# The joins of a triangular block inverse cut down to their 32 and 64 wide blocks, and what moves around them

## The chip, the cores and the metric

One core of a Trainium2 chip runs the whole program. The metric is the time of one execution on the device in microseconds (us); the kernel before has a median of 1515.43 us in 3 runs (1513.37 to 1519.95).

## The reference, cut to what matters

One step of a diffusion backbone: width 1024, two layers, 512 latent tokens and 128 context tokens ("prompt") with the same weights. Layer 0 has a mixer: one input projection, a bidirectional gated DeltaNet with 4 heads of 128 beside a gated short convolution, one output projection. Layer 1 has a pooling mixer. Each layer ends in a gated ConvFFN. The adaLN vectors that modulate everything are `silu(cond) @ w_ada + b_ada`, for two conditions.

The part that the change touches is the triangular solve of the DeltaNet:

```
m = where(strict, einsum("bhncd,bhnsd->bhncs", kb, k) * decay, 0.0)
a = m + eye(CHUNK)
u = triangular_solve(a, vb);  w = triangular_solve(a, kb * exp(gc))
step: v_new = u - w @ s;  o = qg @ s + attn @ v_new;  s = s * gl + kg^T @ v_new
```

The kernel works in chunks of 128 tokens: 5 tiles (4 latent, 1 prompt), 2 directions, 4 heads, so it needs 40 inverses of unit triangular 128x128 matrices before its scan can start.

## The kernel before, in words

Everything is kept with channels on the partitions, tokens along the free axis. Large products are split in high and low parts: a **unit** is one 128 wide block of output channels, 48 matmuls of 128x320 (L686), and needs its weight tile loaded (SP queue, slots `raw`), rounded (`weight_hi` on ACT, L1114, or POOL) and its remainder (`weight_lo` on DVE, L1579, or POOL). The order of all work is written out by hand, one instruction stream for each engine, with semaphores between them.

The input projection is units 0 to 27: 8 of queries and keys, 12 of the short convolution, 4 of values (`U_V`), 4 of the gate (`U_G`, units 24 to 27). Between them DVE does the convolutions, the row sums (below), the products that fill `rinv` with the negated, masked gram matrices (`prepare`), and the inverses of all 32x32 diagonal blocks (`substitute`, L1695 and L1698: the two triangular factors of 4 blocks, 4 heads and all tiles side by side, 30 steps). This runs twice: the prompt's tile first (`lanes_out` at about 271 us), the four latent tiles after it (`lanes_out` at 309 to 313 us).

**The joins.** From the inverses of the diagonal blocks, the full 128x128 inverse comes in two steps, first 32 to 64 and then 64 to 128, as -D C D for each off-diagonal corner C. The kernel before does each with full 128x128 matrices, most of them zeros. ACT spreads the diagonal blocks into cleared buffers (`expand_pair`, 8 small copies per direction and tile, L1186). Then in each of 5 rounds (one tile or pair of tile and direction, both directions): `y5` (L835, 4 matmuls per direction), ACT copies the corners that count (`y5_copy`), `z5` (L845, L847, 8 matmuls), DVE adds (`update_t`, `update_r5`), `y6` (L854), `y6_copy`, `z6` (L862), DVE adds into `rinv` (`update_r6`). An fp32 matmul is two pairs of weight load and matmul instruction in the trace, so each round has 80 such pairs. Transposes of keys and values (`tokens`, L826, copied by ACT L1204) lie between them. The buffers are cleared by DMAs from a tensor of zeros, one of 2 MB.

**Row sums.** `row_sums(n)` (L1498) is the adaLN product for one row tile of 128 outputs: DVE multiplies a loaded 128x1024 tile by the two condition rows, two instructions with accumulation. `ROWS_IN`, `ROWS_B`, `ROWS_JOIN`, `ROWS_OUT` say how many stand where on DVE and `ROWS_LOAD` where their loads stand on the SP queue; a load waits until the sums two tiles earlier are done. Of the first 24, 10 stand in the input projection, 10 in the joins, 4 in the output projection.

**The scan** has 5 steps of both directions: products with the state (L903, L906), DVE (L1820), the product with `rinv` (L913), products with `kg` and the attention (L923, L925), and the state update. POOL scales the keys (`kg`, L646).

Of the kernel before, what the change touches and what calls it, by code (L numbers as in the profile page):

```python
# [26 lines left out]
P = 128  # L27
D = 1024
# [15 lines left out]
ADA_IN = 24  # L44
# [64 lines left out]
ROWS_LATE = ROWS_EARLY + ROWS_JOIN  # L109
assert ROWS_EARLY == 2 + sum(ROWS_LOAD.values()) and ROWS_LATE + sum(ROWS_OUT) == ADA_IN  # L110
# [3 lines left out]
PAIRS = [(NT - 1, 0), (NT - 1, 1)] + [(s if c == 0 else NT - 2 - s, c) for s in range(NT - 1) for c in range(2)]  # L114
# [31 lines left out]
def build(nc, t):  # L146
    ctx = ExitStack()
    with ctx:
# [46 lines left out]
        def heads(ap, n):  # L195
            return [ap[:, 512 * j:512 * (j + 1)].rearrange("p (h e) -> p h e", h=NH) for j in range(n)]
        rdx, ttx = heads(flat[:, 0:2048], 4), heads(flat[:, 2048:4096], 4)
        r5, tt2 = heads(flat[:, 4096:5120], 2), heads(flat[:, 5120:6144], 2)
# [5 lines left out]
        ys6 = nc.alloc_sbuf_tensor_at("ys6", [P, 2, NH, P], F32, offset=x_at + 13 * SLOT)  # L204
        sp_ = nc.alloc_sbuf_tensor_at("sp_", [P, 2, NH, P], F32, offset=x_at + 8 * SLOT)
        row_late = [nc.alloc_sbuf_tensor_at(f"row_late{j}", [P, SLOT], F32, offset=w_at + (2 + j) * SLOT * 4) for j in range(2)]
        cond_late = nc.alloc_sbuf_tensor_at("cond_late", [P, 2, D], F32, offset=w_at)
# [24 lines left out]
        ys5 = nc.alloc_sbuf_tensor_at("ys5", [P, 2, NH, P], F32, offset=o4)  # L232
# [8 lines left out]
        attn_kept = [attn[:, j] for j in range(2 * NT - 4)] + attn_last  # L241
# [124 lines left out]
        s_clear_r = sem("expanded_blocks_cleared")  # L366
        s_clear_y5 = sem("y5_products_cleared")
        s_clear_y6 = sem("y6_products_cleared")
# [4 lines left out]
        s_attn_work = sem("attn_moved_from_work")  # L373
# [3 lines left out]
        s_ex = sem("blocks_expanded")  # L377
# [3 lines left out]
        s_tt2 = sem("tt2_ready")  # L381
        s_r5 = sem("r5_ready")
# [3 lines left out]
        s_rinv = sem("rinv_ready")  # L386
        s_kq = [sem(f"scan_kq{c}") for c in range(2)]
# [26 lines left out]
        def row_buf(n):  # L414

            return (row_late[n % 2] if ROWS_EARLY <= n < ROWS_LATE else ada_raw[n % 2])[:]
# [5 lines left out]
        def row_cond(n):  # L422

            return cond_late if ROWS_EARLY <= n < ROWS_LATE else cond_rows
# [23 lines left out]
        def _(sp):  # L448
# [25 lines left out]
            for u in range(2, 28):  # L474
# [4 lines left out]
                if u == 3:  # L479
                    sp.wait_ge(s_x0, 8)  # L480
                    sp.dma_start(t["x_save"], x[:]).then_inc(s_saved, 16)
                elif u == 4:
                    sp.wait_ge(s_silu_rows, 1)
                    sp.dma_start(t["cond_save"], cond_rows[:]).then_inc(s_cond_saved, 16)
                elif u == U_B + 2:
                    sp.wait_ge(s_saved, 16)
                    sp.wait_ge(s_a, 8)
                    sp.dma_start(d_blk, t["zeros"][:, 0:SLOT]).then_inc(s_clear_d, 16)
                elif u == U_V + 2:
                    sp.wait_ge(s_bc, 2 * NT)  # L490
                    sp.wait_ge(s_row_sums, ROWS_EARLY)
                    sp.wait_ge(s_cond_saved, 16)
                    sp.dma_start(ys5[:].rearrange("p a h e -> p (a h e)"), t["zeros"][:, 0:SLOT]).then_inc(s_clear_y5, 16)
            sp.wait_ge(s_silu, PRIMED + NQKV)
            sp.wait_ge(s_am, 2 * NT)
            sp.dma_start(flat[:, 0:4096], t["zeros"]).then_inc(s_clear_r, 16)
            sp.wait_ge(s_ex, 2)
            sp.dma_start(ys6[:].rearrange("p a h e -> p (a h e)"), t["zeros"][:, 0:SLOT]).then_inc(s_clear_y6, 16)
# [4 lines left out]
            for j in (2, 1, 0):  # L503
                sp.dma_start(attn_kept[j], attn_first[j]).then_inc(s_attn_work, 16)
            sp.dma_start(cond_late[:], t["cond_save"]).then_inc(s_cond_rows, 16)
            for _ in range(2):
                load_rows(rows)
                rows += 1
# [4 lines left out]
            while rows < ROWS_LATE:  # L513
                load_rows(rows)
                rows += 1
            sp.wait_ge(s_ex, 2 * NT)
            sp.dma_start(x[:, 0:3], t["x_save"][:, 0:3]).then_inc(s_back[0], 16)
            sp.wait_ge(s_rinv, 2 * NT)
# [75 lines left out]
        def _(pool):  # L594
# [41 lines left out]
            pool.wait_ge(s_tok, 2 * NT)  # L636
            for s in range(NT):
                for c in range(2):
                    if s == 0:
                        pool.wait_ge(s_rinv, 2 * NT)  # L640
                    else:
                        pool.wait_ge(s_ap[c], s)
# [6 lines left out]
                if s == 0:  # L649
                    u = SEG["out"]["u"]  # L650
                    pool.wait_ge(s_row_sums, ROWS_LATE)
                    pool.wait_ge(s_cond_rows, 32)
# [23 lines left out]
        def _(pe):  # L676
# [120 lines left out]

            for u in range(28):
# [7 lines left out]
                if u == GSUM_AFTER:  # L806
                    gate_sums()
                if u in GRAMS_AFTER:
# [11 lines left out]
            def tokens(i, j):  # L820

                if i:
                    pe.wait_ge(s_tok, 2 * i + j - 1)
                c0 = TILES[PREP[i]]
                for h in range(NH):
                    last = nc.tensor.transpose(bank[6 + j][:, h], qkv[:, 4 + 4 * j + h, c0:c0 + P], ident)  # L826
                last.then_inc(s_tr, 1)

            def y5(l):
                n, c = PAIRS[l]  # L830
                pe.wait_ge(s_ex, l + 1)
                if l >= 2:
                    pe.wait_ge(s_y6c, l - 1)
                for h in range(NH):
                    last = nc.tensor.matmul(bank[c][:, h], rinv[:, 2 * n + c, h], ttx[l % 4][:, h],  # L835
                                            start=True, stop=True)
                last.then_inc(s_y5, 1)

            def z5(l):
                n, c = PAIRS[l]  # L840
                pe.wait_ge(s_y5c, l + 1)
                if l >= 2:
                    pe.wait_ge(s_rinv, l - 1)
                for h in range(NH):
                    nc.tensor.matmul(bank[2 + c][:, h], rdx[l % 4][:, h], ys5[:, c, h], start=True, stop=True)  # L845
                for h in range(NH):
                    last = nc.tensor.matmul(bank[4 + c][:, h], ys5[:, c, h], rdx[l % 4][:, h], start=True, stop=True)  # L847
                last.then_inc(s_z5, 1)

            def y6(l):  # L850
                n, c = PAIRS[l]
                pe.wait_ge(s_tt2, l + 1)
                for h in range(NH):
                    last = nc.tensor.matmul(bank[c][:, h], rinv[:, 2 * n + c, h], tt2[c][:, h], start=True, stop=True)  # L854
                last.then_inc(s_y6, 1)

            def z6(l):
                n, c = PAIRS[l]
                pe.wait_ge(s_y6c, l + 1)
                pe.wait_ge(s_r5, l + 1)  # L860
                for h in range(NH):
# [1220 lines left out]
```

## Time and profile before

| | us |
|---|---|
| median of 3 runs | 1515.43 |
| the profiled execution, own time | 1512.7 |
| its span | 1510.9 |
| TensorE (PE) busy in the span | 1403.6 (93%) |
| VectorE (DVE) busy | 989.8 (66%) |
| units 0 to 27 and what lies between them | 72 to 304 |
| joins, to the first matmul of the scan | 304 to 363 |
| scan | 363 to 417 |

The page gives PE 82% of the chain that ended last. Times in rows are microseconds from the start of the span. In a row of a timeline the first number is the start, the second the time from there to the end of the last instruction that is merged in it, x the count, and the bracket the idle time of the engine before it and what ended it. PEld is the weight load of TensorE, which overlaps the matmuls.

### The profile page before, as it was taken

How to read it: one execution, taken by the hardware profiler on the slowest of the kernel's cores; microseconds unless marked ns; L12 is line 12 of the kernel's file. 1: busy time of each engine (PE TensorE's matmuls, PEld its weight loads, DVE VectorE, ACT ScalarE, POOL GpSimd, SP SyncE). 2: the span in 40 equal slices, each digit the busy share in tenths (PEclk: the TensorE clock that was granted, in tenths of full speed). 3: DMA queues.
4: the chain of work that ended last, by engine and by line, in shares of the span. 5: the costliest groups of instructions: out<-in, count | busy, mean ns of one | idle time of the engine just before them, and what ended most of it. 6: DMA issues, size and time to landing. Idle time of an engine off the chain costs nothing.

```text
span 1510.9 us, 24566 instructions
## 1 busy us (share of the span) xinstructions
PE 1403.6 (93%) x9517; PEld 1366.8 (90%) x9517; DVE 989.8 (66%) x1403; ACT 428.9 (28%) x746; POOL 506.0 (33%) x304
## 2 busy tenths in 40 slices
PE   2699999989879799999999999888999999999996
PEld 1599989988879799999999999778999999999995
DVE  5784688887575777778888886446774155325554
ACT  4734443464421533102210222344110011001122
POOL 0200010003225133453356334112544545455442
PEclk9899999999989999999999999999999999999998
DMA  9342212353032235343434442111332222222222
GB/s 368 126 154 84 98 56 70 122 186 137 9 134 72 85 137 186 126 154 124 150 117 164 139 137 73 54 42 56 111 102 79 70 80 71 73 82 69 69 72 82
DMA packets 44791, 163.24 MB, mean 108 GB/s; under 512 B 4800, under 2 KB 5952, under 8 KB 43584
## 3 DMA queue, kind: packets, MB, share of 16 engines
q1 hardware_dynamic: 44736, 162.52, 31.2%
q8 instruction: 32, 0.52, 0.1%
q14 instruction: 23, 0.19, 0.0%
HBM read 154.12 MB, written 6.82 MB: 107 GB/s over the span
## 4 chain that ended last, share of the span: by engine, by line
PE 82%; DVE 8%; ACT 4%; issue 3%; DMA 2%; ACTq 0%; POOL 0%; DVEq 0%; SPq 0%; POOLq 0%
PE ps L686 72%; PE ps L971 1%; ACT work L1040 1%; ACT work L1186 1%; DMA x<-in_x 1%; PE ps L718 1%; PE ps L794 1%; DMA work<-in_zeros 1%; PE ps L925 1%; PE ps L923 1%; PE ps L913 1%; PE ps L764 1%; PE ps L698 1%; DVE work L1418 1%; DVE work L1478 1%
## 5 line engine op out<-in xcount | busy, mean ns | idle before, releaser
L686 PE MATMUL ps<-hhi,whi 128*128 128x320 f32 x1984 | 458.8, 312 | 31.8 <-DVE hlo L1482 29.9
L686 PE MATMUL ps<-hlo,whi 128*128 128x320 f32 x1984 | 454.0, 310 | 0.0
L686 PE MATMUL ps<-hhi,wlo 128*128 128x320 f32 x1984 | 453.4, 310 | 0.0
L686 PEld LDWEIGHTS ps<-hhi,whi 128*128 128x128 f32 x1984 | 333.5, 189 | 39.8 <-issue 17.8
L686 PEld LDWEIGHTS ps<-hlo,whi 128*128 128x128 f32 x1984 | 334.2, 189 | 0.0
L686 PEld LDWEIGHTS ps<-hhi,wlo 128*128 128x128 f32 x1984 | 334.0, 189 | 0.0
L603 POOL TENSOR_TENSOR wlo<-raw,whi 128x1024 fp32r<-128x1024 f32 (+1 forms) x102 | 255.4, 2504 | 8.5
L600 POOL TENSOR_SCALAR whi<-raw 128x1024 fp32r<-128x1024 f32 (+1 forms) x102 | 105.9, 1039 | 453.3 <-PE ps L686 360.5
L608 POOL TENSOR_TENSOR wlo<-raw,whi 128x1024 fp32r<-128x1024 f32 x44 | 110.7, 2515 | 213.7 <-ACT whi L1389 213.7
L686 PE MATMUL ps<-hidlo,whi 128*128 128x320 f32 x704 | 160.3, 308 | 0.0
L686 PE MATMUL ps<-hidhi,wlo 128*128 128x320 f32 x704 | 160.2, 308 | 0.0
L686 PE MATMUL ps<-hidhi,whi 128*128 128x320 f32 x704 | 160.2, 308 | 0.0
L1396 ACT ACTIVATE work<-ps 128x640 f32<-128x640 f32 x44 | 31.1, 706 | 428.7 <-PE ps L686 428.7
L1923 DVE TENSOR_TENSOR hidlo<-work,hidhi 128x640 fp32r<-128x640 f32 (+1 forms) x44 | 106.7, 2426 | 41.3 <-ACT hidhi L1406 41.3
L1515 DVE SCALAR_TENSOR_TENSOR work<-work,cols 128x511 f32<-128x511 f32 x120 | 122.1, 1058 | 3.7 <-DVE work L1512 0.3
L1512 DVE TENSOR_SCALAR work<-work,cols 128x640 f32<-128x640 f32 x60 | 60.2, 1003 | 97.0 <-ACT work L1396 79.6
L1498 DVE SCALAR_TENSOR_TENSOR ada_raw<-ada_raw,cond_rows 128x1024 bf16<-128x1024 f32 x70 | 121.6, 1738 | 0.0
L686 PEld LDWEIGHTS ps<-hidhi,wlo 128*128 128x128 f32 x704 | 117.8, 188 | 0.0
L686 PEld LDWEIGHTS ps<-hidlo,whi 128*128 128x128 f32 x704 | 117.8, 188 | 0.0
L686 PEld LDWEIGHTS ps<-hidhi,whi 128*128 128x128 f32 x704 | 117.7, 188 | 0.0
L1401 ACT ACTIVATE work<-work 128x640 f32<-128x640 f32 x44 | 32.5, 739 | 217.4 <-DVE work L1521 217.4
L1453 DVE SCALAR_TENSOR_TENSOR x<-ps,mod,x 128x320 f32<-128x320 f32 (+2 forms) x120 | 45.4, 434 | 70.6 <-PE ps L686 70.6
(202 smaller groups left out, 1411.0 us busy)
## 6 DMA issues: line engine op xcount, KB each, us to landing
raw<-in_w_gu SPq DMA_DIRECT2D x88, 512.0 KB, 3.2
ada_raw<-in_w_rows SPq DMA_DIRECT2D x70, 512.0 KB, 3.4
raw<-in_w_in SPq DMA_DIRECT2D x28, 512.0 KB, 3.3
raw<-in_w_dn SPq DMA_DIRECT2D x32, 448.0 KB, 3.3
ada_first<-in_w_ada SPq DMA_DIRECT2D x4, 2048.0 KB, 22.5
raw<-in_w_dn SPq DMA_DIRECT2D x16, 512.0 KB, 3.3
row_late<-in_w_rows SPq DMA_DIRECT2D x10, 512.0 KB, 3.3
raw<-in_w_out SPq DMA_DIRECT2D x8, 512.0 KB, 4.1
```

What stands on the lines that cost most here:

```text
L600: nc.gpsimd.tensor_scalar(whi[s][:, 0:n], raw[s][:, 0:n], 1.0, 0.0, ALU.mult, ALU.add).then_inc(s_whi, 1)
L603: nc.gpsimd.tensor_tensor(wlo[s][:, 0:n], raw[s][:, 0:n], whi[s][:, 0:n].bitcast(F32), ALU.subtract).then_inc(s_split, 1)
L608: nc.gpsimd.tensor_tensor(wlo[s][:], raw[s][:], whi[s][:].bitcast(F32), ALU.subtract).then_inc(s_split, 1)
L686: last = nc.tensor.matmul(pair[pr][:, b], wt[s][:, cs], act[:, k, b * HALF:(b + 1) * HALF], start=(j == 0 and q == 0), stop=(j == len(tile ...
L698: last = nc.tensor.matmul(ada_row(n), c_parts[:, q, 4 * s + k, :], w[:, k * ADA_COLS:(k + 1) * ADA_COLS], start=(s == 0 and k == 0 and q = ...
L1396: nc.scalar.activation(halves(pad[0]), pair["A"], ACT.Copy).then_inc(s_ev["A"], 1)
L1401: nc.scalar.activation(cv[1], cv[0], ACT.Silu).then_inc(s_silu, 1)
L1453: last = nc.vector.scalar_tensor_tensor(out=x[:, k, xc:xc + ln], in0=pair[n][:, bk, pc:pc + ln], scalar=mod[:, layer, 3 * part + 2, k, cd: ...
L1498: last = nc.vector.scalar_tensor_tensor(out=(row_out(n), row_buf(n)[:, 0:SLOT // 2].bitcast(mybir.dt.bfloat16))[c], in0=row_buf(n), scalar ...
L1512: own.tick(nc.vector.tensor_scalar(dst[:, 0:W], src[:, 0:W], taps[1], None, ALU.mult))
L1515: last = nc.vector.scalar_tensor_tensor(out=dst[:, c0 + 1:c0 + n], in0=src[:, c0:c0 + n - 1], scalar=taps[0], in1=dst[:, c0 + 1:c0 + n], o ...
L1923: nc.vector.tensor_tensor(hidlo[:, i, :], h32[0], hidhi[:, i, :].bitcast(F32), ALU.subtract).then_inc(s_hid, 1)
```

## The change

1. **Joins.** The matmuls multiply only blocks: `y5` and `z5` have 32x32 weights and 32 moving columns, `y6` and `z6` have 64 wide weights and 32 moving columns, in turn over 64 rows (the part that was just joined) and over 32 rows (the part that is still a single block). Each tile has 16 + 32 + 16 + 16 = 80 such matmuls for its 4 heads and 2 directions, where it had 40 full ones. Results of both directions and of two tiles stand in one bank. The tiles go in three groups, `JOINS`: the prompt's alone, then (0, 3), then (1, 2).
2. **No expansion, no zeros.** `expand_pair`, its cleared buffers, three DMAs of zeros and the adds go. In their place ACT and DVE copy joined rows and diagonal blocks beside each other (`even_rows`, `odd_rows`, `odd_diagonals`, `even_diagonals`), DVE copies finished parts into `rinv` (`inner_columns`, `outer_corner`), and POOL copies the 32 wide diagonals into it (12 copies, `s_rd`).
3. **Order.** The prompt's group goes between the gate units: `y5(0)` behind unit 24, `z5(0)` behind 25, `y6(0)` behind 26, `z6(0)` behind 27. The other two groups are interleaved with each other, with token transposes between them and six transposes behind them, all of which the scan's first matmul waits for.
4. **Row sums.** None stands in the joins any more: 18 in the input projection, 6 in the output projection, with the SP loads moved alongside, and the 10 loads, their buffers and a copy of the conditions in the joins go. Three attention tiles that were moved out of the work buffer stay where they are.

```diff
-ROWS_IN, ROWS_B = [0, 1, 1, 1, 1, 0, 1, 0], [1, 2, 2]
-ROWS_LOAD = {5: 1, 6: 1, 7: 1, 8: 1, 10: 1, 13: 1, 14: 1, 15: 1}
-ROWS_JOIN, ROWS_OUT = 10, [1, 1, 1, 1, 0, 0, 0, 0]
+ROWS_IN, ROWS_B = [0, 1, 1, 1, 1, 1, 1, 1], [2, 2, 1, 3, 2, 1]
+ROWS_LOAD = {4: 1, 5: 1, 6: 1, 7: 1, 8: 1, 9: 1, 10: 1, 11: 2, 12: 2, 13: 1, 14: 2, 15: 2}
+ROWS_OUT = [1, 1, 1, 1, 1, 1, 0, 0]
+JOINS = [(NT - 1,), (0, 3), (1, 2)]
+TOKENS = [(0, 0), (3, 0), (0, 1), (3, 1), (1, 0), (2, 0), (1, 1), (2, 1), (4, 0), (4, 1)]
...
+            def z5(g):
+                up, low = blocks_of(g)
+                y = join[g][0]
+                out = corner_bank(g).rearrange("p s (t h k) -> p s t h k", h=NH, k=BLOCK)
+                pe.wait_ge(s_y5c, g + 1)
+                for i, n in enumerate(JOINS[g]):
+                    for h in range(NH):
+                        for b in range(0, Q, 2):
+                            for c in range(2):
+                                to_, of = corner(c, b)
+                                r = (up, low)[c][quarter(to_), c, i, h]
+                                nc.tensor.matmul(out[quarter(to_), 1, i, h], r, y[quarter(to_), i, h],
+                                                 start=True, stop=True)
+                                last = nc.tensor.matmul(out[quarter(of), 0, i, h], y[quarter(to_), i, h], r,
+                                                        start=True, stop=True)
+                last.then_inc(s_z5, 1)
...
+            def y6(g):
...
+                for i, n in enumerate(JOINS[g]):
+                    for h in range(NH):
+                        for c in range(2):
+                            f = half(1 - c)
+                            a = rinv[:, 2 * n + c, h]
+                            nc.tensor.matmul(out[f, i, h, BLOCK * c:BLOCK * (c + 1)], a[half(c), f],
+                                             (q, p)[c][half(c), i, 1, h], start=True, stop=True)
+                            one = quarter(1 + c)
+                            last = nc.tensor.matmul(out[f, i, h, BLOCK * (1 - c):BLOCK * (2 - c)], a[one, f],
+                                                    (low, up)[c][one, c, i, h], start=True, stop=True)
+                last.then_inc(s_y6, 1)
...
+                if u >= U_G:
+                    (y5, z5, y6, z6)[u - U_G](0)
...
+            y5(1)
+            y5(2)
+            z5(1)
+            z5(2)
+            tokens(0)
+            tokens(1)
+            y6(1)
+            y6(2)
+            tokens(2)
+            tokens(3)
+            z6(1)
+            z6(2)
+            for j in range(4, 2 * NT):
+                tokens(j)
```

`y5` and `z6` are built like `z5` and `y6`. On DVE the new order is: `some_rows(2)` ahead of `weight_lo(10)`, 2, 1, 3, 2 and 1 sums behind it, one of them between `weight_lo(14)` and the first `scale_qk`; `even_diagonals(0)` behind the first `lanes_out`; `odd_rows(0)` behind `weight_lo(27)` and ahead of the last 17 steps of `substitute`.

## Rows read from the trace of the kernel before

**Rows 1.** Windows by stage: window, its length, busy us (count) of each engine, PEclk, DMA share, GB/s
```profile
72.00:304.00 232.00, 229.00 (x1509) 217.29 (x1509) 173.31 (x322) 95.31 (x173) 12.68 (x10) 1.00 0.29 98
304.00:363.00 59.00, 51.45 (x442) 49.86 (x441) 48.01 (x87) 35.34 (x105) 0.00 (x0) 1.00 0.47 161
```

**Rows 2.** Timeline of PE in the joins: the first waits, one round, the scan
```profile
304.85 2.02 PE L835 MATMUL ps<-work,rinv 128*128 128x128 f32 x16 [0.84 <-issue]
...
314.04 2.05 PE L854 MATMUL ps<-work,rinv 128*128 128x128 f32 x16 [3.15 <-DVE work L1714]
...
319.92 1.16 PE L835 MATMUL ps<-work,rinv 128*128 128x128 f32 x8 [0.50 <-ACT work L1186]
320.91 0.60 PE L826 MATMUL ps<-const,qkv 128*128 128x128 f32 x4
321.35 1.06 PE L845 MATMUL ps<-ys,work 128*128 128x128 f32 x8
...
362.98 1.13 PE L903 MATMUL ps<-ss,qkv 128*128 128x128 f32 x8 [1.35 <-issue]
```

**Rows 3.** The chain that ended last, in order of time: start, us, what
```profile
131.19 7.24 PE ps L686 x48
...
140.59 7.04 PE ps L686 x48
...
325.09 1.94 PE ps L854 x16
```

**Rows 4.** Timeline of PE around the transposes of 16 rows (L752)
```profile
130.33 0.46 PE L686 MATMUL ps<-hhi,wlo 128*128 128x320 f32 x2
130.72 0.48 PE L752 MATMUL ps<-const,work 16*128 16x16 f32 x5
131.12 0.56 PE L686 MATMUL ps<-hhi,whi 128*128 128x320 f32 x2
```

**Rows 5.** Timeline of the weight loads at the same place, and of the loads of L709
```profile
130.71 0.38 PEld L752 LDWEIGHTS ps<-const,work 16*128 16x128 f32 x5 [0.19 <-issue]
131.12 0.30 PEld L686 LDWEIGHTS ps<-hhi,whi 128*128 128x128 f32 x2
...
34.49 0.52 PEld L709 LDWEIGHTS ps<-cols,ada_rows 4*128 4x128 f32 x4 [0.23 <-issue]
```

**Rows 6.** Groups of weight loads by shape: busy us, mean ns of one
```profile
L835 PEld LDWEIGHTS ps<-work,rinv 128*128 128x128 f32 x80 | 9.6, 191 | 4.0 <-ACT work L1186 3.0 <-issue 1.1
L698 PEld LDWEIGHTS ps<-more,c_parts 128*4 128x4 f32 x64 | 4.8, 84 | 5.3 <-DVE more L1568 3.8
L752 PEld LDWEIGHTS ps<-const,work 16*128 16x128 f32 x5 | 0.4, 136 | 0.2 <-issue 0.2
```

**Rows 7.** Timeline of DVE and PE where the first grams wait
```profile
175.32 0.82 DVE L1632 TENSOR_TENSOR work<-work,ps 128x640 f32<-128x640 f32 x1 [6.35 <-PE ps L686]
182.35 1.23 DVE L1498 SCALAR_TENSOR_TENSOR junk<-ada_raw,cond_rows 128x1024 bf16<-128x1024 f32 x1
194.66 2.05 PE L794 MATMUL ps<-qkv 128*128 128x128 f32 x16 [2.55 <-DVE qkv L1624]
```

**Rows 8.** Timeline of DVE from the gate units to the end of the block inverses
```profile
273.86 1.22 DVE L1579 TENSOR_TENSOR wlo<-raw,whi 128x1024 fp32r<-128x1024 f32 x1
295.42 1.23 DVE L1579 TENSOR_TENSOR wlo<-raw,whi 128x1024 fp32r<-128x1024 f32 x1 [3.29 <-ACT whi L1114]
311.55 1.89 DVE L1705 STREAM_TRANSPOSE blocks<-blocks 128x1024 f32<-128x1024 f32 x1
```

**Rows 9.** Timeline of ACT and DVE: one token copy, the memsets ahead of the scan
```profile
321.68 0.60 ACT L1204 ACTIVATE ktok<-ps 128x512 f32<-128x512 f32 x1
365.22 1.03 DVE L1812 MEMSET sp__55<- 128x512 f32 x2
```

**Rows 10.** Timeline of DVE in the output projection; DMA issues: KB, us to landing
```profile
465.19 1.14 DVE L1453 SCALAR_TENSOR_TENSOR x<-ps,mod,x 128x320 f32<-128x320 f32 x3 [0.35 <-PE ps L686]
472.30 1.13 DVE L1453 SCALAR_TENSOR_TENSOR x<-ps,mod,x 128x320 f32<-128x320 f32 x3 [2.42 <-PE ps L686]
raw<-in_w_out SPq DMA_DIRECT2D x8, 512.0 KB, 4.1
```

More of the change, by code:

```diff
@@ new lines, in y6 @@
+            def y6(g):
+                up, low = blocks_of(g)
+                p, q = join[g][1:3]
+                out = join_bank(g, 2, 256).rearrange("p (t h k) -> p t h k", h=NH, k=64)
+                pe.wait_ge(s_ep, g + 1)
+                pe.wait_ge(s_eq, g + 1)
+                pe.wait_ge(s_pd, g + 1)
+                for i, n in enumerate(JOINS[g]):
+                    for h in range(NH):
+                        for c in range(2):
+                            f = half(1 - c)
[6 more added lines that the diff above has]
+                last.then_inc(s_y6, 1)
@@ new lines, in z6 @@
+            def z6(g):
+                up, low = blocks_of(g)
+                p, q, y = join[g][1:4]
+                out = join_bank(g, 3, 256).rearrange("p (t h k) -> p t h k", h=NH, k=64)
+                pe.wait_ge(s_y6c, g + 1)
+                for i, n in enumerate(JOINS[g]):
+                    for h in range(NH):
+                        for c in range(2):
+                            f, to_ = half(1 - c), half(c)
+                            nc.tensor.matmul(out[to_, i, h, BLOCK * (1 - c):BLOCK * (2 - c)], y[f, i, h],
+                                             (p, q)[c][f, i, 0, h], start=True, stop=True)
+                            one = quarter(2 - c)
+                            last = nc.tensor.matmul(out[to_, i, h, BLOCK * c:BLOCK * (c + 1)], y[one, i, h],
+                                                    (up, low)[c][one, c, i, h], start=True, stop=True)
+                last.then_inc(s_z6, 1)
@@ L850, in y6 @@
[L850 to L861, printed above, removed]
-                    last = nc.tensor.matmul(bank[4 + c][:, h], ys6[:, c, h], r5[c][:, h], start=True, stop=True)
-                last.then_inc(s_z6, 1)
+            y5(1)
@@ new lines, in even_diagonals, with odd_rows @@
+            def even_diagonals(g):
+                _, low = blocks_of(g)
+                dve.wait_ge(s_blk, 1 if g == 0 else 2)
+                for q in (0, 2):
+                    for c in range(2):
+                        nc.vector.tensor_copy(join[g][2][quarter(q), :, 1 - c], low[quarter(q), c])
+            def odd_rows(g):
+                dve.wait_ge(s_z5, g + 1)
+                for q in (1, 3):
+                    last = nc.vector.tensor_copy(join[g][2][quarter(q)].rearrange("p t s h k -> p s t (h k)"),
+                                                 corner_bank(g, quarter(q)).rearrange("p s (t e) -> p s t e", e=P))
+                last.then_inc(s_eq, 1)
```

355 lines of the change are left out of this document (165 added, 190 removed).

## The prediction

> **What bounds the kernel now.** The windows by stage come first [rows 1]. From 72 to 304 us PE is busy 229 of 232 us: the input projection is bound by PE. In the joins, 304 to 363 us, PE is busy 51.5 of 59.0 us at full granted clock, DVE 48.0, ACT 35.3. So the joins are a PE stage too, with some holes. The timeline of PE shows which [rows 2]: 0.84 us before the first join (so the last unit ends at 304.01), 3.15 us in the first round, 0.5 to 0.57 us in each of the four later rounds (one stands in the rows), and 1.35 us before the scan, which starts at 362.98. The chain of waits runs over PE's own matmuls in a round [rows 3]; DVE with its ten row sums and ACT with its expansions lie beside them. A change of the joins is therefore worth what it takes from PE's instructions and these holes, and not what it takes from DVE, ACT and the DMAs.
>
> **What one round costs PE now.** y6 of both directions, 16 pairs of weight load and matmul, takes 1.79 to 1.94 us [rows 3], 0.112 us a pair. A round has 80 such pairs, 8.9 us, and two token transposes of 0.44 us; five rounds are 44.6 us.
>
> **The joins in blocks.** The change doubles the number of matmuls: 80 for a tile, 160 pairs. Everything turns on two prices, and the trace of before has no 32 wide matmul.
>
> First the pair. The smallest matmuls that it has are the five transposes of 16 rows with 16 moving columns: their weight loads start within 0.38 us, and one lasts 0.136 [rows 5, 6], so the step is (0.38 - 0.136)/4 = 0.061 us. That is about 0.0625 us for a pair in which the matmul itself is tiny. Bound above: the full pair, 0.112 us. Bound below: the weight loads go from 84 ns for 4 columns to 191 ns for 128 [rows 6], 0.86 ns a column, so 32 columns take 28 ns; moving 32 columns where 128 need at most 112 ns also gives 28 ns. A pair can't be under 0.03 us, or 0.055 with 64 weight columns. I take 0.0625: it is the nearest row in size and the loads there already fetch few bytes.
>
> The Trainium skill ("TensorEngine Tiling (Array Packing)", Instruction Overhead) says that each matmul has an overhead of some 60 cycles, below which fewer columns gain nothing. By it an estimate from that page is 25 ns for each instruction of a pair at 2.4 GHz, 0.05 us a pair, a tile of 8 us without changes and 1499 us for the kernel; the step of 0.061 us in this trace speaks for more.
>
> Second the change of shape. Before the first 16-row matmul PE goes 0.24 us from the last start (two merged units start 0.147 apart, so the last at 130.48, then 130.72) instead of 0.147 [rows 4], and the weight loads show 0.19 us of idle put down to issue [rows 5]. The unit behind them takes 7.24 us instead of 7.04 [rows 3]. The stretch of the five costs 0.40 + 0.20 = 0.60 us; five steps of 0.0625 are 0.31; 0.29 is left for two changes. L709, with 4 rows, has the same idle time before its loads, 0.23 us [rows 5]. So changing between a full and a 32-row matmul costs 0.1 to 0.15 us. In the new y6 and z6, matmuls of 64 and 32 rows alternate: 32 changes for a tile. No row shows a change between these two; bounds 0 and 0.2 us, and I take 0.11, the low side of the measured one.
>
> The same page of the Trainium skill (Key Properties) says that a change of the tiling mode drains TensorE, while a change of tile does not. The rows around L752 agree with it, with 0.1 to 0.15 us each, and by it the alternation in y6 and z6 is charged.
>
> A tile then costs 160 x 0.0625 + 32 x 0.11 = 10.0 + 3.5 = 13.5 us of PE, against 8.9 before.
>
> **The prompt's group between gate units.** PE is full there [rows 1], so its 13.5 us push the end of unit 27 back one for one, with 8 changes between full and block shapes, 0.9 us: 14.4. It is not hidden, it is paid earlier. Its partners are in time: the first block inverse is out at about 271 us, y5(0) runs after 282, and every copy on ACT and DVE has a unit of 7 us to finish in.
>
> **The second block inverse.** It ends on DVE at 311.55 + 1.89 = 313.4 us [rows 8]. The 3.29 us in which DVE waited for ACT (held by the DMA of zeros) go; odd_rows(0) puts DVE behind z5(0), 0.6 us and some waiting. I get about 312, against 317 for PE's end of z6(0): PE is last. Were pairs at 0.03 us, this inverse would be last.
>
> **The rest of the joins.** Four tiles, 54.0 us. Tokens: twice two transposes, 0.9 us each time; six at the end with two banks, where a bank's next transpose waits for ACT's copy of 0.60 us [rows 9]: 3.5 us to the last one and 0.8 to its copy, 4.3 in all. Sum 60.1 us. ACT's and DVE's new copies, about 30 of 0.3 to 0.6 us, and POOL's 12 small ones, lie beside PE: with two groups interleaved each has a partner's matmuls as cover. Without it each of four hand-overs would add about 0.8 us. The scan's first step loses a stall: rr no longer queues behind a row sum and the memsets (365.22 for 1.03 us [rows 9], while kq of the first direction is done at about 364.8): -0.9.
>
> **Row sums.** In the input projection eight more sums of 2.3 us go into DVE's idle time before 175.32, of which the last piece alone is 6.35 us [rows 7]; their loads, 3.3 to 4 us to land, hold the SP queue behind the sums, but I find each weight tile landed at least 3 us before it is rounded. One tile fewer stands between the last weight_lo and scale_qk (now two, the second at 182.35): -2.3 us on the path to the grams, where PE waits 2.55 [rows 7]. The sums in front of body_conv(1) make it late by about 0.8: net -1.5. The four copies behind the first lanes_out push weight_lo(24), which has 0.8 us to spare (273.86 + 1.2, unit 24 begins at 275.8) [rows 8]: +0.3. Together -1.2, between -2.5 and +1. In the output projection two more sums fall into k = 4 and 5, where DVE has 0.35 to 2.42 us idle before an update [rows 10] and one add of squares that is stretched; PE needs raw tile 5 some 2 us later than it would then be split (4.1 us to land): 0, at worst +2. The DMAs that go, the expansions and the attention moves: 0, as their only stall on the path was DVE's 3.29 us.
>
> **Sum.** From 304.01: -1.2 + 14.4 + 60.1 = 73.3 us to the scan, against 59.0: +14.3, less 0.9 gives +13.4 us. On the profiled execution's own time, 1512.7 (span 1510.9), that is 1526.1; I say 1526. The median of the runs shown is 2.7 above that execution, so part of what is measured may be that.
>
> **Rivals.**
> A. Pairs at 0.0625 us, but a change between 64 and 32 rows is free. A tile is 10.0 us: -1.2 + 10.0 + 0.9 + 40.0 + 6.1 = 55.8 against 59.0, less 0.9: -4.1, 1509. For it: only changes from and to the full height are seen. Against: the 0.19 us of idle looks like a wait for the array to be empty, which two heights would need too. Pairs of 0.04 us with the changes charged end at the same place (6.4 + 3.5 = 9.9).
> B. The other side: the array's own time sets the step, and blocks in different corners overlap. y5 and z5 96 x 0.03, y6 and z6 64 x 0.055: 6.4 us a tile. PE would be done with the prompt at 310, the block inverse ends last at 312; then 25.6 + 6.1: the scan starts at 343.7, -19.3, less 0.9: -20.2, 1492.5. For it: full pairs run at what 128 columns take, and not above. Against: the step of 0.061 us for nearly nothing to multiply. The sign turns at a tile of (59.0 + 1.2 + 0.9 - 0.9 - 6.1)/5 = 10.8 us: stage of before, row sums, scan, less changes around the prompt's group and tokens.
> C. A pair costs the full 0.112 us whatever its size, as fp32 loads of 128 columns do: 17.9 + 3.5 = 21.4 a tile, +53 us, 1566. Milder: PE's clock is granted low for part of the joins because the array is mostly empty, +5 to +15 on top of the forecast.
>
> **How the numbers follow.** Forecast 0.44, A 0.22, B 0.22, C 0.12. The forecast's own range, with a tile of 12 to 15 us, is 1518 to 1534; the range for 8 in 10 takes in A, B's figure and the milder C: 1492 to 1542. What a measurement tells from no change is 0.5%, 7.6 us. Slower: C and most of the forecast, 0.12 + 0.38 = 0.50. Faster: B and a part of A, 0.22 + 0.09 = 0.31. Same: 0.19.
>
> **What would show it.** Step between weight loads in y5 and z5: 0.06 us (0.03 is B, 0.11 is C). In y6 and z6, if matmuls go by twos with about 0.23 us a two-pair product, the changes are paid; with 0.125, it is A. Group 0: behind the gate units stand 2.2, 4.2, 4.0 and 4.0 us of joins. Scan's start at 376 us; PE's wait before the first grams 1 us or less; no PE wait in units 4 to 7 of the output projection; PEclk at full in the joins. I am wrong if the joins after unit 27 take under 50 us.

## The result, and the profile after

The changed kernel takes 1535.45 us (median of 4 runs, 1533.46 to 1538.95) against 1516.49 for the kernel before on the same chip: 19.0 us slower by the medians, and a ratio of 1.0134 with a 95% interval of 1.0119 to 1.0149, which is 20.3 us. The sign and the range of the prediction hold; the size does not: 0.9% over 1512.7 was forecast with +13.4 us, and 19.0 came. (The forecast of 1526 us itself stands only 9.5 us above 1516.49, half of what came, since it was added to one execution that lay 3.8 us under that median.) The profiled execution after took 1538.95 us, 3.5 above its median, while the one before lay 3.8 below its own. The two traces are therefore 26.2 us apart where the medians are 19.0, and a figure that stands on the two traces alone is to be read with that in mind.

The row of the granted clock on the page, by slices of 38 us, first:

```profile
PEclk9899999955989999999999999998999999999998
```

Two slices of the 40 stand at 5 (307 to 384 us), where the joins are. The windows of this stretch (window, its length, busy us of each engine with counts, granted clock, DMA share, GB/s) answer to [rows 1]:

```profile
305.00:310.00 5.00, 5.00 (x25) 5.00 (x25) 4.46 (x16) 0.39 (x1) 0.00 (x0) 0.66 0.00 0
310.00:320.00 10.00, 10.00 (x204) 9.02 (x207) 9.18 (x18) 1.09 (x2) 3.64 (x8) 0.80 0.39 134
320.00:330.00 10.00, 6.23 (x276) 5.36 (x270) 4.20 (x10) 6.43 (x11) 0.00 (x0) 0.50 0.02 5
330.00:340.00 10.00, 10.00 (x59) 8.14 (x60) 0.87 (x3) 0.00 (x0) 0.00 (x0) 0.50 0.00 0
...
360.00:370.00 10.00, 10.00 (x59) 8.14 (x60) 1.38 (x2) 0.00 (x0) 0.00 (x0) 0.50 0.01 2
```

PE is never idle from 330 to 370 us (two of the four windows are shown), VectorE and ScalarE have next to nothing to do, and PE starts only 59 matmuls in 10 us, at 1.2 GHz (0.50) where the kernel before had 2.4 GHz throughout [rows 1]. The clock is already low at 305 to 310, in the unit behind y6(0), without any idle time before it. It is back at 1.00 when z6(0) starts (313.75), falls again inside z6(0) at 316, and stays at 0.50 until the scan.

The timeline of PE in y5(0), y6(0), y6(1), and at the end of the joins shows what a product costs (start, duration, line, names, shapes, machine matmuls merged in a row):

```profile
285.79 0.21 PE L830 MATMUL ps<-blocks,rinv 32*32 32x32 f32 x1
285.80 0.21 PE L830 MATMUL ps<-r_blk,rinv 32*32 32x32 f32 x1
...
286.05 0.19 PE L830 MATMUL ps<-r_blk,rinv 32*32 32x32 f32 x1
286.17 0.41 PE L700 MATMUL ps<-hhi,whi 128*128 128x320 f32 x1
...
301.33 0.30 PE L866 MATMUL ps<-work,rinv 64*64 64x32 f32 x2
301.56 0.30 PE L869 MATMUL ps<-blocks,rinv 32*64 32x32 f32 x2
...
335.76 0.42 PE L866 MATMUL ps<-work,rinv 64*64 64x32 f32 x2
336.10 0.41 PE L869 MATMUL ps<-rt_late,rinv 32*64 32x32 f32 x2
...
381.45 0.79 PE L965 MATMUL ps<-ss,qkv 128*128 128x128 f32 x5 [0.78 <-ACT vtok L1260]
```

The 32 pairs of y5(0) start within 0.26 us, 8 ns from one to the next. A product of y6 (one matmul of the program, two pairs in the trace) comes every 0.23 us at full clock and every 0.345 us at half clock. The scan starts at 381.45 us, 18.5 later than before [rows 2].

PE's waits before the scan (L808 are the first grams, L847 stands in z5) and, in a second view, in the output projection (us in all, times, longest):

```profile
PE ps L808 <- DVE qkv L1671: 3.8, 1, 3.8
PE ps L847 <- issue: 3.8, 2, 1.9
...
PE ps L700 <- POOL wlo L609: 4.6, 3, 2.7
```

The wait at the first grams is 3.8 us against 2.55 [rows 7], and behind it the grams run at a low clock: 16 matmuls in 3.79 us against 2.05. Unit 15 starts 2.3 us later than before. The timeline of VectorE shows why, and what became of the sums in the output projection:

```profile
166.57 1.23 DVE L1545 SCALAR_TENSOR_TENSOR junk<-ada_raw,cond_rows 128x1024 bf16<-128x1024 f32 x1 [2.07 <-DMA ada_raw<-in_w_rows]
...
183.03 2.06 DVE L1545 SCALAR_TENSOR_TENSOR ada_raw<-ada_raw,cond_rows 128x1024 bf16<-128x1024 f32 x1
...
479.75 2.06 DVE L1545 SCALAR_TENSOR_TENSOR junk<-ada_raw,cond_rows 128x1024 bf16<-128x1024 f32 x1
481.74 3.41 DVE L1545 SCALAR_TENSOR_TENSOR ada_raw<-ada_raw,cond_rows 128x1024 bf16<-128x1024 f32 x1
485.08 1.12 DVE L1500 SCALAR_TENSOR_TENSOR x<-ps,mod,x 128x320 f32<-128x320 f32 x3
```

VectorE waits for the row tiles themselves (2.07 us here, 2.67 at 175.04), and a half of a sum that takes 1.22 us elsewhere takes 2.06 to 3.41 here. GpSimd's two steps of a split, on its own timeline, are longer at the same time too, 1.69 and 3.24 us against 1.05 and 2.35 where no sum runs beside them:

```profile
479.05 1.69 POOL L606 TENSOR_SCALAR whi<-raw 128x1024 fp32r<-128x1024 f32 x1 [2.81 <-DMA raw<-in_w_out]
480.82 3.24 POOL L609 TENSOR_TENSOR wlo<-raw,whi 128x1024 fp32r<-128x1024 f32 x1
490.45 1.05 POOL L606 TENSOR_SCALAR whi<-raw 128x1024 fp32r<-128x1024 f32 x1 [6.39 <-DMA raw<-in_w_out]
491.58 2.35 POOL L609 TENSOR_TENSOR wlo<-raw,whi 128x1024 fp32r<-128x1024 f32 x1
```

The chain of waits in the output projection says who pays (start, us, what):

```profile
479.75 2.07 DVE junk L1545 x2
481.82 2.13 DVE ada_raw L1545
...
485.56 4.63 DMA raw<-in_w_out
```

SyncE holds the load of the next weight tile behind that of a row tile, which waits for the sum; GpSimd splits the weight late, and PE waits for the split. From the start of the scan to the end of the span the changed kernel takes 1155.8 us in this trace, the kernel before 1147.9.

### The profile page after: what moved, and what is told of

It is laid out like the page before. It is cut to its first block, busy times and chain, and to the rows that moved or that the text cites. A ratio compares the mean times of both kernels' runs of the same rounds, so it can differ in the third digit from the quotient of the medians.

```text
span 1537.2 us, 25228 instructions
## 1 busy us (share of the span) xinstructions
PE 1430.5 (93%) x9917; PEld 1380.1 (90%) x9917; DVE 990.2 (64%) x1409; ACT 404.4 (26%) x654; POOL 513.5 (33%) x316
## 4 chain that ended last, share of the span: by engine, by line
PE 83%; DVE 8%; ACT 3%; issue 3%; DMA 2%; POOL 0%; ACTq 0%; DVEq 0%; SPq 0%; POOLq 0%
PE ps L700 71%; PE ps L1033 2%; ACT work L1102 1%; DVE ada_raw L1545 1%; DVE junk L1545 1%; PE ps L883 1%; PE ps L886 1%; PE ps L866 1%; PE ps L869 1%; PE ps L808 1%; PE ps L732 1%; PE ps L922 1%; DMA x<-in_x 1%; DMA ada_raw<-in_w_rows 1%; PE ps L987 1%
## 5 line engine op out<-in xcount | busy, mean ns | idle before, releaser
L1545 DVE SCALAR_TENSOR_TENSOR ada_raw<-ada_raw,cond_rows 128x1024 bf16<-128x1024 f32 x80 | 139.9, 1748 | 0.0
L1545 DVE SCALAR_TENSOR_TENSOR junk<-ada_raw,cond_rows 128x1024 bf16<-128x1024 f32 x80 | 99.7, 1246 | 6.4 <-DMA ada_raw<-in_w_rows 4.7
```

What stands on the lines that cost most here:

```text
L1545: last = nc.vector.scalar_tensor_tensor(out=(row_out(n), row_buf(n)[:, 0:SLOT // 2].bitcast(mybir.dt.bfloat16))[c], in0=row_buf(n), scalar ...
```

## Experiments

All numbers are against the kernel before, run on the same chip in between. Kernels of one group of four shared these runs. The medians: by_shape 1503.74, by_head 1511.14, same_corner 1545.05, rows_only 1520.79 (before 1516.32); fill_waits 1498.61, fill_all 1507.69, tokens_early 1501.63, rows_back 1495.18 (before 1516.29); after_fill 1538.9, after_rows 1530.04, best 1495.49, best_late 1491.45 (before 1514.93).

### The order of the two shapes: by_shape and by_head

```
y6 and z6, by_shape:
+ for part in range(2):                # 0: 64 rows, 1: 32 rows
      for i, n in enumerate(JOINS[g]):
          for h in range(NH):
              for c in range(2):
                  ... the product of this part alone
by_head: for i / for h / for part in range(2) / for c
```

> The changed kernel with the products of y6 and z6 in another order: first all those of 64 rows, then all those of 32 rows (two shapes, one change between them in each function, in place of one at every product). Nothing else moves. Theory, that the alternation of the two shapes is what the joins pay for, by itself (0.2275 us a product of two pairs at full clock) and by a granted clock of 0.50 that follows it: y6(0) falls from 3.65 us to about 1, y6 and z6 of the two groups from 22 us each to 4 to 8, the clock no longer falls at 305 to 310, and the kernel takes 25 to 45 us less than the changed one (1490 to 1510). Rival, that pairs of 64 and 32 rows cost this much by themselves and the clock falls because of the waits for VectorE in the joins: under 3 us less, still 0.23 us a product.

> The changed kernel with y6 and z6 taken per head: two products of 64 rows, then two of 32 rows, so half the changes of shape. Theory (each change of shape has a price): y6(0) about 2 us in place of 3.65, the two groups' y6 and z6 10 to 15 us each in place of 22, the kernel 10 to 22 us under the changed one. If the price were the pair's and not the change's: no change in time. If only the low clock mattered and it needs fewer changes to come: between the two, with the clock at 0.50 and a product that costs no less.

by_shape: 1503.74 us, ratio 0.9926 (0.9907 to 0.9944), 31.7 us under the changed kernel and faster than the kernel before. by_head: 1511.14, ratio 0.9973 (0.996 to 0.9985), 24.3 under the changed kernel, a little more than the upper end of 22 that was expected. PE's timeline of y6(0) in by_shape:

```profile
301.98 0.66 PE L869 MATMUL ps<-work,rinv 64*64 64x32 f32 x16
302.56 0.24 PE L872 MATMUL ps<-blocks,rinv 32*64 32x32 f32 x1
...
303.14 0.56 PE L700 MATMUL ps<-hhi,whi 128*128 128x320 f32 x2
```

The same 32 pairs take 1.16 us with one change of shape in place of 3.65 with 15, so 14 alternations cost 2.49 us, 0.18 us each, if what neighbours of one shape gain by overlapping (the 32-row pairs here lie in two corners and start by twos) is put down to them. by_head stands between: with 7 changes its y6(0) takes 1.87 us (301.83 to 303.70), so the first six more cost 0.12 us each and the last eight, which also part the pairs of neighbours, 0.22. The mean is therefore not the price of a change alone. The windows of by_shape:

```profile
305.00:310.00 5.00, 5.00 (x36) 5.00 (x35) 4.49 (x16) 0.00 (x0) 0.00 (x0) 1.00 0.00 0
310.00:320.00 10.00, 5.22 (x316) 4.74 (x315) 9.47 (x21) 3.98 (x7) 3.66 (x8) 0.65 0.40 134
320.00:330.00 10.00, 7.82 (x210) 7.16 (x194) 5.07 (x12) 4.14 (x7) 0.00 (x0) 0.50 0.02 4
330.00:340.00 10.00, 10.00 (x154) 9.41 (x154) 1.34 (x2) 1.79 (x3) 0.00 (x0) 0.50 0.01 3
```

The clock no longer falls behind y6(0). It still falls at 313, where PE waits 3.1 us for the second block inverse behind z6(0) (from 311.6 to 314.7), and stays low until 347. At half clock y6 of the two groups takes 7.4 us (325.55 to 332.94) and z6 7.4, against 22.2 each; in by_head they take 11.3 each. The rival, that pairs of these shapes are dear by themselves, falls.

### Neighbours in one corner: same_corner

```
y5 and z5:
- for i, n in enumerate(JOINS[g]): / for h / for b / for c
+ for b / for c / (z5: for part) / for i, n in enumerate(JOINS[g]): / for h
```

> The changed kernel with the 32-row products of y5 and z5 ordered so that all products of one 32x32 corner of the array stand in a row (in the changed kernel neighbours lie in different corners, 8 to 15 ns from start to start). Theory, that neighbours in different corners overlap: the step grows to 30 to 60 ns, 448 products more by 0.02 to 0.05 us each, together 9 to 20 us over the changed kernel. Rival, that a product of 32 rows and 32 columns is this short wherever it lies: the same time within 2 us. Since z5's two products of a pair stand apart here, the order inside z5 changes too.

1545.05 us, ratio 1.020 (1.018 to 1.022), 9.6 us over the changed kernel, at the low end of the theory. y5(0) begins and ends:

```profile
286.30 0.34 PE L830 MATMUL ps<-blocks,rinv 32*32 32x32 f32 x5
...
286.88 0.32 PE L830 MATMUL ps<-r_blk,rinv 32*32 32x32 f32 x5
287.12 0.56 PE L700 MATMUL ps<-hhi,whi 128*128 128x320 f32 x2
```

The unit behind it starts 0.82 us after y5(0) in place of 0.38: 32 pairs are 0.44 us, or 14 ns each, dearer, so some 22 ns from one to the next in place of 8. The 9.6 us hold more than is seen at once: the two holes of PE in z5 (3.8 us in the changed kernel) are gone, so the dearer pairs cost more than 9.6. Neighbours in different corners of the array do overlap; this is rival B's mechanism, at a price well under its 30 ns. The Trainium skill ("TensorEngine Tiling (Array Packing)", Instruction Overhead) has some 60 cycles for each matmul, 25 ns as an estimate from that page. Counted once for a pair it is near the step of 22 ns within one corner; counted for each instruction of a pair, as the prediction did (0.05 us), it is too much, and the 8 ns between corners lie under it either way.

### The row sums alone: rows_only and after_rows

```
rows_only, against the kernel before:
- ROWS_IN, ROWS_B = [0, 1, 1, 1, 1, 0, 1, 0], [1, 2, 2]
- ROWS_JOIN, ROWS_OUT = 10, [1, 1, 1, 1, 0, 0, 0, 0]
+ ROWS_IN, ROWS_B = [0, 1, 1, 1, 1, 1, 1, 1], [2, 2, 1, 3, 2, 1]
+ ROWS_JOIN, ROWS_OUT = 0, [1, 1, 1, 1, 1, 1, 0, 0]
after_rows, against the changed kernel (5 rows in two buffers of the weight parts, free then):
+ ROWS_IN, ROWS_B = [0, 1, 1, 1, 1, 1, 1, 1], [2, 2, 1, 2, 1, 0]
+ ROWS_JOIN, ROWS_OUT = 5, [1, 1, 1, 1, 0, 0, 0, 0]
  ...            # in both kernels the loads of the rows move alongside
  inner_columns(2)
+ some_rows(4)
  outer_corner(1)
+ some_rows(1)
```

> The kernel before with the row sums alone placed as in the changed kernel (none in the joins, more before the first grams and two more in the output projection, the shift added at the seventh row). Theory from the changed kernel's trace: slower than the kernel before by 6 to 10 us, of which 2 to 3 before unit 15 (sums that wait for their rows and then run at 2 us beside GpSimd) and 6 to 7 in the output projection (sums of up to 3.4 us in front of the weight splits). Rival, the forecast (row sums hidden in slack): 0 to 3 us faster.

rows_only: 1520.79 us, ratio 1.0028 (1.0016 to 1.0039), 4.5 us over the kernel before. PE's waits, for GpSimd in the output projection and for VectorE at the first grams:

```profile
PE ps L680 <- POOL wlo L599: 4.4, 2, 2.8
...
PE ps L788 <- DVE qkv L1618: 3.6, 1, 3.6
```

Before they were 1.6 and 2.55 us. By the traces unit 15 starts 2.2 us later than before (200.71 against 198.52), the joins 2.3 later (307.15 against 304.85), the scan 1.6 later (364.60), and from there to the end of the span it takes 3.6 us more. So the 2 to 3 us before unit 15 came as expected, and of the 6 to 7 in the output projection about half. The theory had 6 to 10 us, from the trace of one execution of the changed kernel; the cost is real, and smaller. The forecast of a gain falls.

> The changed kernel with the row sums placed as in rows_back and nothing else: the joins' y6 and z6 alternate as in the changed kernel. Theory (the placement of the row sums costs its own part, whatever the joins do): 6 to 10 us under the changed kernel, as rows_back lay 8.6 under by_shape. Rival, that the 4.5 us that rows_only showed are all there is: 4 to 5 under. If the sums' loads delay the joins, under 3.

after_rows: 1530.04 us, ratio 1.0105 (1.0079 to 1.0131), 5.4 us under the changed kernel by the medians, 4.4 by the ratios. That fits the rival, which took the 4.5 us of rows_only for all there is. The wait at the first grams is gone and the one for GpSimd is back at 1.6 us, but PE's holes in z5 grow from 3.8 to 6.5 us, and the unit behind y6(0) takes 9.8 us where it took 8.8, since the clock falls earlier; so what the two projections win is partly lost again in the joins.

### What brings the clock down: fill_waits, fill_all, after_fill

```
+ fill(12)     # matmuls 128 x 128 x 512 into a free bank, their result is not used
  y5(1)
  y5(2)
+ fill(4)
  z5(1)
+ fill(8)
  z5(2)
+ fill(8)
fill_all: also fill(2) before each block of 8 products of y6 and z6
after_fill: the fills of fill_waits in the changed kernel
```

> The kernel by_shape with matmuls that serve nothing (128 rows and columns, 512 elements, into a bank that is free then) in PE's waits of the joins after unit 27: 12 before y5(1), 4 before z5(1), 8 before z5(2), 8 behind it. In by_shape the granted clock falls to 0.50 at 312 us, in a wait of 3.1 us behind z6(0), and stays there to 347. Theory, that the clock falls because the array has too little full-size work in these microseconds: it stays at 1.00 until 325 at least, and the time falls by 3 to 12 us (if y6 and z6 too then run at full clock, by some 12; if the clock falls inside them, by 3). Rival, that the small shapes alone bring the clock down, whatever stands between them: 0.50 from 312 on all the same, and the time is the same or up to 6 us more.

fill_waits: 1498.61 us, ratio 0.9893 (0.9874 to 0.9911), 5.1 us under by_shape. Its windows:

```profile
310.00:320.00 10.00, 8.38 (x308) 6.63 (x307) 9.61 (x21) 4.14 (x8) 3.65 (x8) 1.00 0.39 134
320.00:330.00 10.00, 9.29 (x252) 7.87 (x252) 4.97 (x12) 3.89 (x7) 0.00 (x0) 1.00 0.02 6
330.00:340.00 10.00, 9.76 (x184) 8.75 (x183) 3.72 (x6) 3.50 (x7) 1.91 (x6) 0.83 0.11 19
```

The clock stays at 1.00 through y6 and most of z6, for work that is of no use: the theory holds. y6 takes 4.2 us and z6 4.5 in place of 7.4 each.

> The kernel fill_waits with two more such matmuls ahead of each block of 8 products of y6 and z6 of the two groups (16 blocks, 32 matmuls of some 0.22 us at full clock, 7 us in all). Theory (full-size work holds the clock): 1.00 through the joins, so that their 7.1 us each for y6 and z6 come down to 3.5 and the ten token groups to half, 12 us gained against 7 paid: 2 to 6 us under fill_waits if the clock falls there in y6, 5 to 8 over it if it held there already. Rival (small shapes bring it down anyway): 0.50 all the same, 12 to 15 us over by_shape.

fill_all: 1507.69 us, ratio 0.9946 (0.9926 to 0.9966), 9.1 us over fill_waits by the medians and 8.0 by the ratios, at the upper end of the 5 to 8 expected for a clock that was held already. The additional matmuls cost their time and more changes of shape: a block of 8 products comes every 1.25 us, 0.59 of it its own.

> The changed kernel, its y6 and z6 still alternating between 64 and 32 rows, with the 32 matmuls that serve nothing of fill_waits in PE's waits of the joins. It parts the two costs of the alternation. Theory (each change of shape costs its price, and the low clock comes from too little full-size work): the clock is at 1.00 where the joins begin; if it stays there, the 64 products each of y6 and z6 take 0.2275 us in place of 0.345, 15 us less than the changed kernel's, about 1520. If the alternation itself brings the clock down again inside y6 (as at 305 in the changed kernel, behind y6(0)), only 2 to 6 us less, 1530 to 1534. If the fillers did nothing: 0 to 6 more.

after_fill: 1538.9 us, ratio 1.0164 (1.0137 to 1.019): 3.5 us over the changed kernel by the medians, 4.5 by the ratios. None of the gains came; the time is that of fillers that do nothing, though the trace shows that they did something. Its windows, and two products at full clock:

```profile
320.00:330.00 10.00, 9.19 (x406) 7.14 (x405) 2.50 (x4) 5.58 (x10) 0.00 (x0) 1.00 0.02 6
330.00:340.00 10.00, 10.00 (x75) 8.16 (x74) 2.56 (x9) 1.14 (x3) 0.00 (x0) 0.82 0.01 2
340.00:350.00 10.00, 10.00 (x59) 8.13 (x59) 0.00 (x0) 0.60 (x1) 0.00 (x0) 0.50 0.00 0
```
```profile
334.15 0.30 PE L869 MATMUL ps<-blocks,rinv 32*64 32x32 f32 x2
334.38 0.30 PE L866 MATMUL ps<-work,rinv 64*64 64x32 f32 x2
```

The same fillers that hold the clock in front of products in order bring it to 1.00 here too, up to 336 us; then it falls to 0.50 inside the alternating products of y6, with PE busy all the time and no wait before it. So the alternation costs twice: 0.23 us a product, and a low clock that makes it 0.345. Whether the changes themselves bring the clock down, or only the longer stretch without full-size work that they make (y6 of the two groups lasts some 20 us here and 4.2 in fill_waits), no run parts.

### Placing it better: tokens_early, rows_back, best, best_late

```
tokens_early: tokens(0), y5(1), y5(2), z5(1), tokens(1), z5(2), tokens(2), y6(1), tokens(3),
              y6(2), tokens(4), z6(1), tokens(5), z6(2), tokens(6..9)
rows_back:    by_shape with the rows of after_rows
best:         rows_back with 3, 1, 2, 2 fills (f32, from the constant tile)
best_late:    best, and on SyncE:
+ sp.wait_ge(s_z5, 3)
  sp.dma_start(cond_late[:], t["cond_save"]).then_inc(s_cond_rows, 16)
  while rows < ROWS_LATE: load_rows(rows) ...
```

> The kernel by_shape with the groups of four token transposes (128 rows and columns, real work) placed one by one in the joins: one before y5(1), one behind z5(1), z5(2), y6(1), y6(2), z6(1), and four at the end in place of six. Where the joins of by_shape end with six groups at 0.85 us each behind z6, two of them move into waits: 2 to 4 us less. If spreading full-size work also keeps the granted clock up for part of the joins: 6 to 15 less. Rival, that the copies of the groups on ScalarE delay the even rows and y6's copies: within 1 us of by_shape.

tokens_early: 1501.63 us, ratio 0.9913 (0.9893 to 0.9933), 2.1 under by_shape, the low end of the 2 to 4 expected; the clock is 0.50 from 320 to 345 all the same, so single groups of four transposes don't hold it.

> The kernel by_shape with eight of its row sums put back or moved: 15 early (by_shape 18), 5 in the joins where VectorE idles for 11 us in by_shape, 4 in the output projection (by_shape 6). Theory, that the placement of the row sums costs what rows_only showed against the kernel before (4.5 us): 3 to 6 us under by_shape, most of it in the output projection, with waits for GpSimd's splits back to 1 to 2 us. Rival, that the sums in the joins delay the corner copies or the start of the scan, or that the splits are late by themselves: same as by_shape within 1 us.

Five sums move here, not eight: three out of the input projection and two out of the output projection. rows_back: 1495.18 us, ratio 0.9865 (0.9848 to 0.9883), 8.6 under by_shape, more than the expected 3 to 6. In the profiled executions the wait before the first grams (3.5 us in by_shape) is gone and PE's wait for GpSimd's splits is 1.6 us in place of 4.6. But PE's two holes in z5, 3.8 us in all in by_shape, have grown to 6.8. PE's waits in the joins, and PE (busy, clock, DMA share, GB/s) around the hole:

```profile
PE ps L862 <- issue: 6.8, 2, 4.6
```
```profile
313.00:314.00 1.00, 0.00 (x0) 0.50 1.01 401
314.00:315.00 1.00, 0.00 (x0) 0.50 1.08 410
```

> The kernel rows_back (products by shape, row sums moved) with full-size matmuls that serve nothing in PE's waits of the joins: 3 before y5(1), 1 before z5(1), 2 before z5(2), 2 behind it, here in f32 from the constant tile. If the gains of fill_waits (5 us) and of rows_back (8.6 us) add: 1490. In rows_back PE idles 4.6 us inside z5 with nothing that the profile names, while the loads of the row tiles move 400 GB/s; these fillers come before and behind it, so the clock may fall in it all the same: then 1493 to 1496.

best: 1495.49 us, ratio 0.9874 (0.985 to 0.9897). The gains did not add; by the median nothing came of the fillers, though y6 and z6 of the two groups ran at full clock (y6 4.2 us, 325.17 to 329.37, in place of 7.4). The view of PE's waits names two reasons:

```profile
PE ps L862 <- issue: 4.1, 1, 4.1
...
PE ps L995 <- DVE rinv L1811: 3.1, 1, 3.1
```

The hole stands, and since y6 and z6 now are done before the row sums behind which the corner copies wait, PE waits for VectorE.

> The kernel best with the loads of the second copy of the conditions and of the row tiles for the joins held until z5 is through. Theory, that PE starves of instructions in z5 (its own are fetched by DMA, 256 of them in one packet group, and the row loads stand in their way): the gap of 4.6 us inside z5 goes back to 1 to 2, 2 to 4 us under best. Rival, that the gap has another cause, or that VectorE then waits for its row tiles and the corner copies come late: the same as best, or up to 3 us over.

```profile
PE ps L993 <- DVE rinv L1809: 1.4, 1, 1.4
PE ps L860 <- issue: 1.2, 2, 0.9
```

best_late: 1491.45 us, ratio 0.9858 (0.9828 to 0.9887). The intervals of best and best_late overlap, so the 4.0 us between the medians (2.4 by the ratios) lean on the traces: the hole goes from 4.1 us to 1.2 in two, the longer 0.9, when no bulk transfer runs beside z5. It is the fastest kernel of this study, 44.0 us under the changed one by the medians.

## Why the prediction was right in sign and wrong in size

**The step that failed is "Row sums".** It said -1.2 us before the gate units and 0, at worst +2, in the output projection. Measured alone they cost 4.5 us (rows_only), and moving five of them back gains 4.4 to 5.4 (after_rows). That is 5.6 to 6.6 us off, and the miss of the whole is 19.0 - 13.4 = 5.6. Both halves failed: in the trace of rows_only unit 15 starts 2.2 us late where the input projection was to win 1.2, PE waits 3.6 us at the first grams where 2.3 of 2.55 were to go, and it waits 2.8 us more for GpSimd in the output projection where nothing was charged. The step took a sum for 2.3 us wherever it stands, and looked for idle time of VectorE. It did not ask what runs on GpSimd and the DMA queues at that time: halves of a sum took up to 3.41 us, VectorE waited 2 to 2.7 us for row tiles, and on SyncE the load of the next weight tile stood behind that of a row tile.

**The joins came out right by luck, by sizes that cancel.** With the row sums apart, 19.0 less 4.5 is 14.5 us, and the prediction had 13.4 + 1.2 = 14.6 for them. Its terms were not right:
- Pairs of y5 and z5: 62.5 ns were taken, with 30 as the least that was possible, and 8 ns is what they took at full clock. For the four tiles 24.0 us were charged; y5 and z5 end 8.8 us after unit 27's group (318.18 to 326.99), 3.8 of these the two holes. The price was taken from the nearest row in size, of transposes that all lie in one place of the array; it holds for no pair in another corner than its neighbour, and even within one corner same_corner has 22 ns.
- Changes between 64 and 32 rows: 0.11 us each with a pair of 0.0625 gave 0.235 us a product; 0.2275 was measured. By parts it is 0.12 to 0.22 for the change (by_head, by_shape) and less for the pair.
- The clock was taken as full in the joins, and its fall was kept for the milder C, +5 to +15. It came: 128 products at 0.345 us are 44.2 us where 29.1 would have stood at full clock, 15.1 us more, and the unit behind y6(0) took 8.78 us.
- Tokens: 10.2 us (1.90, 1.90 and 6.35) against 6.1, at the low clock.
- The second block inverse was set at 312 us. PE of by_shape waits for it until 314.7, so it came later than forecast; in the changed kernel PE itself is not there before 318.1, and it costs nothing.
- The prompt's group between gate units: the traces have 11.4 us (unit 24 starts 2.8 us late, the last group ends 14.2 late) against 14.4.

Together 63.3 us from the start of y5(1) to the scan, against the 60.1 of the forecast; the kernel before has 59.0 from its last unit to the scan [rows 2]. Of the 0.9 us for the stall in the scan's first step 0.6 came, in rows_only too: from the first product with the state to the first with `rinv` 3.64 us in place of 4.24.

**Rivals.** A (changes of shape are free) falls with by_shape, and C's pair of 0.112 us with the steps of 8 and 22 ns. B's mechanism is real, but in y5 and z5 only, as long as y6 and z6 alternate; with products in order it decides, and the kernel is faster than before. Of C, the milder form took place beside the forecast, and not in place of it. The rule that the mode change drains TensorE (the Trainium skill, "TensorEngine Tiling (Array Packing)", Key Properties), by which the changes were charged, agrees with these runs in that a change has a price, 0.12 to 0.22 us each; that it is a drain, no trace shows.

**The tests named beforehand.** y6 went by twos at 0.23 us, as said, and the joins after unit 27 took over 50 us. Behind the gate units stood 0.4, 0.7, 3.6 and 4.4 us of joins, where 2.2, 4.2, 4.0 and 4.0 were named: the first two show the pair and not the sum. The step in y5 and z5 was under B's 0.03, the scan started at 381 and not 376, PE waited 3.8 us before the first grams and not 1, it waited behind unit 5 of the output projection (494.17 us, two units before the end), and PEclk was not full. The tests caught what the near sum of the joins hides.

**Open.** Why the clock falls where it does is not settled beyond this: full-size work in the waits kept it up, and with the alternating products it fell while PE was busy. That the holes in z5 are PE waiting for its own instructions was tried by best_late alone, and the traces bear it out. Eleven kernels have 19 holes there of more than 0.6 us, up to 4.6, and each of them ends 1.2 to 1.5 us after a packet of 16 KB of the queue `q8 instruction` has landed (in the changed kernel landed at 321.78 and 325.35, PE goes on at 323.18 and 326.64; in rows_back landed at 315.70, on at 316.90). In same_corner, where the pairs of z5 follow each other more slowly, there is no hole. In best_late the only transfers left beside z5 are those of the instruction queue. What is not shown is why the packet starts 2.4 us after PE ran dry in rows_back (314.70 against 312.32), beside transfers that fill the DMA engines, and 0.5 us before it in the changed kernel (320.82 against 321.31). Why rows_back gained 8.6 us and after_rows 4.4 to 5.4 was not tried further; the unit behind y6(0), slower by 1 us in after_rows, is a part of it.

## What to carry to other kernels

When small matmuls of several shapes are to be issued, sort them by shape (the same 32 pairs took 1.16 us in place of 3.65), and within a shape let neighbours lie in different parts of the array (8 ns from one to the next in place of 22). Price work for an "idle" engine by what runs beside it on its neighbour and in its DMA queue, and look what load stands behind its load. And where a sum comes out right, check its terms: here a pair eight times too dear hid a clock at half speed, and by_shape then gained 31.7 us by the order of two loops.

## What was not expected of the hardware

- 32x32 f32 pairs in different corners start 8 ns apart at 2.4 GHz, in one corner about 22 ns.
- In alternating 64-row and 32-row matmuls, and in the unit behind them, the granted clock fell from 1.00 to 0.50 while PE was busy without a gap (after_fill at 336 us, the changed kernel at 305 and 316); full-size matmuls whose result nobody uses, 32 of some 0.25 us, kept it at 1.00 and made the kernel 5.1 us faster.
- PE ran dry in z5 with no releaser that the profile shows: 1.9 us twice in the changed kernel, 4.6 us at once while the DMAs moved some 400 GB/s beside it, and 0.9 at most with no bulk transfer beside it. Each such hole ended 1.2 to 1.5 us after a packet of the instruction queue had landed.
- A VectorE pass of 1.22 us over 128x1024 took 2.06 to 3.41 us while GpSimd worked beside it, and GpSimd's split steps 1.69 and 3.24 us in place of 1.05 and 2.35: each is slower beside the other.
